# One projection block of a hybrid trunk, cut into eight pieces of k and placed inside the delta-rule scan's last chunk

## The chip, the cores and the metric

The kernel runs on one NeuronCore of a Trainium2 chip. Its time is the device time in microseconds (us) of one execution. All inputs are float32, and every matmul of this kernel appears in the trace as two instructions. Five engines work side by side, each with its own instruction queue, and wait for each other through semaphores: TensorE (PE; its weight loads are shown apart as PEld), VectorE (DVE), ScalarE (ACT), GpSimd (POOL) and SyncE (SP), which streams the weights.

## The reference

Two layers (`DEPTH = 2`), each on 512 latent and 128 context tokens (T = 640 columns) with D = 1024. What matters here, cut down:

```
h = rmsnorm(x, norm_mix_w[l]) * (1 + sc_a) + sh_a
(m_cq, m_ckv, m_kpe, g_q, g_k, g_v, g_z, g_a, g_b, hy_u, d_q, d_k, d_v, z_gate) = split(h @ w_in[l])
o_a = mla_attend(...m_cq, m_ckv, m_kpe...)       # latent attention
o_b, s_gdn = gdn_branch(...)                     # chunked gated delta rule, both directions
o_c = hyena_branch(...) ; o_d = diff_attend(...)

# inside gdn_branch, for each chunk of 64 tokens (kb = k*beta):
a_mat = I + strict_lower(kb k^T * decay)         # is inverted, here by doubling
v_new = u - w state ; o = q e^g state + intra v_new
state = state e^g_last + k^T v_new
# after the last chunk:
o_b = rmsnorm(o, norm_w) * silu(z)
x = x + gt_a * (sum_n sigmoid(gate_n) * (o_n @ w_branch[n])) @ w_out ; then a squared-ReLU MLP
```

## The kernel before

Activations lie transposed, 128 channels by 640 tokens. The input projection `h @ w_in` is cut into 24 blocks of 128 output channels. `win_block(l, n)` computes block n: it waits for its weights in one of four ring slots (`landed`), for the evacuation of an earlier block, and runs `dense`: for each of eight pieces of k (128 input channels each) one matmul over 512 and one over 128 columns, into one half of `psD`, a PSUM tile of two halves with two banks each. The last matmul raises `block_done`; ACT copies the half out (`evac` and its kin) and raises `dense_out`. Before, block n uses half `n % 2`. From block 2 on, block n waits for `dense_out` number n-1, which says that blocks 0 to n-2 have been copied out.

The order on every engine is the order in which the code is written. On PE a layer starts with `hyena` (blocks 0 to 7) and `gdn` (blocks 8 to 14), then come blocks 15 to 17 and `mla` (blocks 18 to 23).

Inside `gdn`, five scan steps (chunks) are worked off; steps 0 to 3 go in pairs, so that PE works on one while DVE works on the other. Step 4 is alone. For each step the inverse of a 64 x 64 lower triangle is made by doubling. A level k has, on PE, `lower_times(s, k)` (L1038); on DVE `w_masked` (L2234), which masks its result; on PE `inverse_times(s, k)` in two halves (L1050 and L1058), which waits for that; and on DVE `inverse_less` (L2244) and `turned_less` (L2254, for the last level L2263), which subtract them. `lower_times(s, k+1)` waits for `inverse_less(s, k)`. After level 5 come `corner_lower` (L1069), ACT's `corner_in` (L1703), `corner_inverse` (L1081) and ACT's `corner_out` (L1713).

The **tail** of step 4 is a chain: `new_values(4)` (L1107), ACT's copy `values_in` (L1718), `outputs(4)` (L1127 and L1133), and DVE's `collect(4)` (L2282, L2293), which raises `scan_done` number 5. The step uses `psA` for the doubling and half 0 of `psD` (`free_bank`, `out_bank`) for the tail. Half 1 of `psD` is in use by the scan (`pair_of`) until `query_keys(4)` has read it, which raises `at_ready` number 5, well ahead of step 4's doubling.

After `scan_done` PE runs block 14, then the **branch sum** (L1254, eight matmul instructions: the sum of squares for the branch's norm), then block 15. The **norm chain** starts at the branch sum: on ACT the logarithm (L1749), a table load and the exponential (L1750), on DVE two products (L2408, L2409); the second raises `gdn_done`. ACT waits for `gdn_done` before it evacuates block 14 (L1550), since the target lies in memory that the branch has used till then. Block 16 on PE waits for that evacuation, `dense_out` number 15:

```
            def mla(l):
                act.wait_ge(*gdn_done.nth(l, 1))
                act.wait_ge(*stored.nth(l, 1))
                evac(l, 14, m_cq[:, 0])
                evac(l, 15, m_cq[:, 1])
```

Of the kernel before, what the change touches and what calls it, by code (L numbers as in the profile page):

```python
# [17 lines left out]
ACT = mybir.ActivationFunctionType  # L18
# [4 lines left out]
KC = D // P  # L23
DEPTH = 2
LAT, CTX = 512, 128
T = LAT + CTX
# [3 lines left out]
KEYS = LAT + 128 + CTX  # L30
# [13 lines left out]
N_GROUP = 2 * KC + N_EARLY // GROUPS  # L44

BRANCHES = (1, 2, 0, 3)
N_FLOW = 24
PACK = 4
N_TURN = N_LATE + N_EARLY // PACK
# [88 lines left out]
def trunk(nc, ins, outs, links):  # L138
    ctx = ExitStack()
    with ctx:  # L140
# [327 lines left out]
        def length_banks(c):  # L468
            b = 2 * ((c + 1) % 2)
            return psA[:, b:b + 2, :].rearrange("p b n -> p (b n)")  # L470

        def tiles_of(s):

            return (s, 3 - s) if s < 4 else (4, 4)
# [246 lines left out]
        def _(pe):  # L721
            mm = nc.tensor.matmul

            def dense(out, j, rhs, ready=None):
                for k in range(KC):
                    if ready:
                        pe.wait_ge(*ready(k))
                    for a, b in SEGS:
                        last = mm(out[:, a:b], ring[:, j, k, :], rhs[:, k, a:b], start=k == 0, stop=k == KC - 1)  # L729
                return last  # L730
# [44 lines left out]
            def norm_sum(l, at_end):  # L775
# [5 lines left out]
                    last = mm(psD[:, 0, a:b], c_("ones"), h[:, KC - 1, a:b], start=False, stop=True)  # L781
                last.then_inc(sumsq_done.sem, 1)

            def win_block(l, n):

                j = n % RING
                landed(l, n)
                if n >= 2:
                    pe.wait_ge(*dense_out.nth(l, n - 1))
                dense(psD[:, n % 2], j, h, (lambda k: h_ready.nth(l, k + 1)) if n == 0 else None)\  # L790
                    .then_inc(block_done.sem, 1)

            for _ in range(RING):
# [128 lines left out]
            def gdn(l):  # L922
# [104 lines left out]
                def lower_times(s, k):  # L1027

                    i = s % 2
                    if k:  # L1030
                        held(pe, *xi_in[i].nth(l, turn_no(s, 6, k)))
                    else:
                        held(pe, *lt_ready.nth(l, s + 1))
                    for d, hh in units:
                        u = d * 4 + hh
                        for r in range(2):
                            mv = xi[i][rows(r), u] if k else c_("identc", rows(r))
                            last = mm(psA[rows(r), 2 * i, u * 64:(u + 1) * 64], lt[s % 3][rows(r), d, hh, rows(r)], mv,  # L1038
                                      start=True, stop=True)
                    last.then_inc(w_ps[i].sem, 1)  # L1040

                def inverse_times(s, k):

                    i = s % 2
                    held(pe, *wm_in[i].nth(l, turn_no(s, 6, k + 1)))
                    if k:
                        held(pe, *xt_in[i].nth(l, turn_no(s, 6, k)))
                        for u in range(8):
                            for r in range(2):
                                last = mm(psA[rows(r), 2 * i, u * 64:(u + 1) * 64], xt[i][rows(r), u], wm[i][rows(r), u],  # L1050
                                          start=True, stop=True)
                        last.then_inc(xi_ps[i].sem, 1)
                    elif s >= 2:
                        held(pe, *xtf_in.nth(l, s - 1))
                    for u in range(8):
                        for r in range(2):
                            mv = xt[i][rows(r), u] if k else c_("identc", rows(r))
                            last = mm(psA[rows(r), 2 * i + 1, u * 64:(u + 1) * 64], wm[i][rows(r), u], mv,  # L1058
                                      start=True, stop=True)
                    last.then_inc(xt_ps[i].sem, 1)  # L1060
# [170 lines left out]
                inverse_times(4, 1)  # L1231
                new_values(3)
                lower_times(4, 2)
                inverse_times(4, 2)
                outputs(3)
                lower_times(4, 3)
                inverse_times(4, 3)
                lower_times(4, 4)
                inverse_times(4, 4)
                lower_times(4, 5)  # L1240
                inverse_times(4, 5)
                corner_lower(4)
                corner_inverse(4)
                new_values(4)
                outputs(4)

                pe.wait_ge(*scan_done.nth(l, 5))
                win_block(l, 14)

                pe.wait_ge(*osq_ready.nth(l, 1))  # L1250
                for c in range(2):
# [272 lines left out]
            with pe.Fori(0, DEPTH) as l:  # L1524
                hyena(l)
                pe.wait_ge(*hy_done.nth(l, 1))
                gdn(l)
                win_block(l, 15)
                for n in range(16, 18):
                    win_block(l, n)  # L1530
                mla(l)
                attention(l)
                merge(l)
                out_proj(l)
                pe.wait_ge(*residual.nth(l, 7))
                norm_sum(l, 0)
                mlp(l)
                pe.wait_ge(*residual.nth(l, 39))
                norm_sum(l, 1)
# [3 lines left out]
        def _(act):  # L1543
# [3 lines left out]
            def evac(l, n, dst):  # L1547

                act.wait_ge(*block_done.nth(l, n + 1))
                a(dst, psD[:, n % 2, 0:T], ACT.Copy).then_inc(dense_out.sem, 1)  # L1550

            def evac_conv(l, n):

# [275 lines left out]
# [5 lines that stand above are left out]

                for n, dst in ((16, m_ckv), (17, kpe)):
                    act.wait_ge(*block_done.nth(l, n + 1))
                    a(dst[:, 0:LAT], psD[:, n % 2, 0:LAT], ACT.Copy)
                    a(dst[:, T:KEYS], psD[:, n % 2, LAT:T], ACT.Copy).then_inc(dense_out.sem, 1)
                act.wait_ge(*dense_out.nth(l, 18))
                a(m_sq[:, 0:2], m_cq, ACT.Square)  # L1840
                a(m_sq[:, 2, 0:LAT], m_ckv[:, 0:LAT], ACT.Square)
                a(m_sq[:, 2, LAT:T], m_ckv[:, T:KEYS], ACT.Square).then_inc(mla_sq.sem, 1)
                for n in (18, 19):
                    evac(l, n, d_q[:, n - 18])
                for n, wd in enumerate((256, 128)):
                    act.wait_ge(*mla_sum.nth(l, n + 1))
                    src = psA[:, 2 * n:2 * n + 2, :].rearrange("p b n -> p (b n)")[:, 0:T]
                    chain.link(a(m_rs[:, n], src, ACT.Ln, scale=1.0 / wd, bias=c_("eps")))
                for n in range(2):
                    a(m_rs[:, n], m_rs[:, n], ACT.Exp, scale=-0.5).then_inc(mla_rs.sem, 1)  # L1850
                for n in (20, 21):
                    act.wait_ge(*block_done.nth(l, n + 1))
                    a(d_k[:, n - 20, 0:LAT], psD[:, n % 2, 0:LAT], ACT.Copy)
                    a(d_k[:, n - 20, T:KEYS], psD[:, n % 2, LAT:T], ACT.Copy).then_inc(dense_out.sem, 1)
                for hh in range(H):
                    act.wait_ge(*mla_q_ps.nth(l, hh + 1))
                    a(m_q[0:96, hh], psD[0:96, hh % 2, 0:T], ACT.Copy).then_inc(mla_q_in.sem, 1)
                for hh in range(H):
                    act.wait_ge(*mla_k_ps.nth(l, hh + 1))
                    a(m_k[0:64, hh], psD[0:64, hh % 2, 0:KEYS], ACT.Copy).then_inc(mla_k_in.sem, 1)  # L1860
                for n in range(3):
                    act.wait_ge(*mla_v_ps.nth(l, n + 1))
                    a(m_v[:, 2 * n:2 * n + 2], psA[:, n, :].rearrange("p (t c) -> p t c", t=2), ACT.Copy)\
                        .then_inc(mla_v_in.sem, 1)
                a(d_k[:, :, LAT:T], p_("dk_c").rearrange("p (c t) -> p c t", c=2), ACT.Copy)
                a(d_v[:, 4], p_("dv_c"), ACT.Copy)
                act.wait_ge(*lam_sum.nth(l, 1))
                a(lam_s[:, 68:70], lam_s[:, 64:66], ACT.Exp).then_inc(lam_exp.sem, 1)
                act.wait_ge(*rot_in.nth(l, 1))
                a(m_k[64:96], kpe[64:96].unsqueeze(1).to_broadcast([32, H, KEYS]), ACT.Copy)\  # L1870
                    .then_inc(mla_k_rope.sem, 1)
                evac(l, 22, d_vf[:, 0])
                act.wait_ge(*rot_in.nth(l, 4))
                for c in range(KC):
                    a(h_high[:, c], h[:, c], ACT.Copy).then_inc(h_high_in.sem, 1)
                evac(l, 23, d_vf[:, 1])
                act.wait_ge(*stored.nth(l, 3))
                act.wait_ge(*rot_in.nth(l, 5))
                act.wait_ge(*mla_k_rope.nth(l, 1))
                high_part(l, B_GATE, 0)  # L1880
# [965 lines left out]
```

## Time and profile before

| what | value |
|---|---|
| median of 3 runs | 3095.86 us (3094.11 to 3096.72) |
| profiled execution, its own time | 3100.46 us |
| its span, first to last instruction | 3098.9 us |
| PE busy / PEld busy | 94% / 78% of the span |
| DVE / ACT / POOL busy | 34% / 26% / 21% |
| share of PE in the chain that ended last | 89% |
| mean granted TensorE clock | 0.976 of full speed |

The time of the profiled execution is 1.6 us longer than its span (what lies around the first and last instruction) and 4.6 us above the median of the runs without a profile. Times in the views are counted from the start of the span. "idle" in brackets is how long the engine stood before the row's first instruction, and behind the arrow stands the instruction that released it. PEclk 1.00 is 2.4 GHz, 0.50 is 1.2 GHz.

### The profile page before, as it was taken

The page shows a single profiled execution, that of the slowest core. Times are in us where ns is not written, and L with a number is a line of the kernel's source. Part 1 is how long each engine was busy: PE and PEld are TensorE (multiplying, and loading weights), DVE is VectorE, ACT ScalarE, POOL GpSimd, SP SyncE. Part 2 cuts the span into 40 slices and gives each one's busy share as a digit, 9 for nine tenths or more (in the row PEclk, how much of TensorE's full clock was granted, in tenths as well). Part 3 has the DMA queues.
Part 4 walks back from the last instruction along what each step waited for, and adds up shares of the span by engine and source line. Part 5 has one row for each costly group of instructions (what it writes and reads, how often), then busy time and mean ns, then how long its engine had stood idle before and what let it go on. Part 6 is the DMA issues. An engine that isn't in the chain of part 4 may idle for free.

```text
span 3098.9 us, 55916 instructions
## 1 busy us (share of the span) xinstructions
PE 2907.4 (94%) x23136; PEld 2426.2 (78%) x23136; DVE 1058.2 (34%) x1984; ACT 809.3 (26%) x1214; POOL 656.1 (21%) x428
## 2 busy tenths in 40 slices
PE   6999999999999899999989998999999998999997
PEld 3558855777778799999956697567777788999997
DVE  1546613224543331111244574132355324111113
ACT  2131023222331241221221411232233214221222
POOL 0102102111212323333301110021121122333332
PEclk9999999999999999999999999999999999999999
DMA  7110011222124222323230100112221232222222
GB/s 301 38 43 10 3 43 36 77 77 77 62 77 135 96 75 90 96 83 96 83 135 25 42 4 10 52 48 77 77 77 63 100 112 90 83 96 89 89 91 81
DMA packets 56671, 235.54 MB, mean 76 GB/s; under 512 B 6624, under 2 KB 6784, under 8 KB 55136
## 3 DMA queue, kind: packets, MB, share of 16 engines
q1 hardware_dynamic: 53568, 206.67, 20.2%
q0 software_dynamic: 2848, 25.13, 2.2%
q8 instruction: 202, 3.31, 0.4%
q14 instruction: 53, 0.43, 0.0%
HBM read 222.96 MB, written 8.81 MB: 75 GB/s over the span
## 4 chain that ended last, share of the span: by engine, by line
PE 89%; DVE 4%; issue 3%; ACT 2%; DMA 1%; POOL 0%; SPq 0%; DVEq 0%; POOLq 0%; ACTq 0%
PE ps_dense L736 47%; PE ps_dense L729 13%; PE ps_dense L1261 4%; PE ps_aux L1312 3%; PE ps_dense L1333 2%; PE ps_aux L1058 2%; PE ps_aux L1038 2%; PE ps_aux L1050 2%; PE ps_aux L1261 1%; PE ps_aux L759 1%; DMA w_ring<-in_w_early 1%; PE ps_dense L1324 1%; PE ps_dense L759 1%; PE ps_dense L1107 1%; PE ps_dense L1399 1%
## 5 line engine op out<-in xcount | busy, mean ns | idle before, releaser
L657 POOL TENSOR_TENSOR w_low<-w_ring,w_high 128x1024 fp32r<-128x1024 f32 x208 | 512.6, 2465 | 1089.4 <-ACT w_high L1566 1087.9
L736 PE MATMUL ps_dense<-h_high,w_high 128*128 128x320 f32 x2048 | 491.8, 321 | 55.5 <-DVE h_low L1979 21.8
L736 PE MATMUL ps_dense<-h_high,w_low 128*128 128x320 f32 x2048 | 468.9, 310 | 0.0
L736 PE MATMUL ps_dense<-h_low,w_high 128*128 128x320 f32 x2048 | 468.7, 310 | 0.0
L729 PE MATMUL ps_dense<-h_norm,w_ring 128*128 128x512 f32 (+1 forms) x1536 | 434.7, 444 | 18.7 <-ACT h_norm L1591 10.6
L729 PEld LDWEIGHTS ps_dense<-h_norm,w_ring 128*128 128x128 f32 x1536 | 240.3, 195 | 217.7 <-issue 206.7
L736 PEld LDWEIGHTS ps_dense<-h_high,w_high 128*128 128x128 f32 x2048 | 336.5, 190 | 79.1 <-issue 44.0
L1566 ACT ACTIVATE w_high<-w_ring 128x1024 fp32r<-128x1024 f32 x208 | 218.9, 1053 | 534.2 <-PE ps_dense L736 433.5
L736 PEld LDWEIGHTS ps_dense<-h_low,w_high 128*128 128x128 f32 x2048 | 344.9, 189 | 0.0
L736 PEld LDWEIGHTS ps_dense<-h_high,w_low 128*128 128x128 f32 x2048 | 344.4, 189 | 0.0
L736 PE MATMUL ps_dense<-z_high,w_high 128*128 128x320 f32 x1280 | 296.5, 313 | 13.5 <-POOL w_low L657 13.5
L736 PE MATMUL ps_dense<-z_low,w_high 128*128 128x320 f32 x1280 | 293.8, 311 | 0.0
L736 PE MATMUL ps_dense<-z_high,w_low 128*128 128x320 f32 x1280 | 293.3, 310 | 0.0
L736 PEld LDWEIGHTS ps_dense<-z_high,w_high 128*128 128x128 f32 x1280 | 215.1, 190 | 16.9 <-issue 16.9
L736 PEld LDWEIGHTS ps_dense<-z_low,w_high 128*128 128x128 f32 x1280 | 216.0, 190 | 0.0
L736 PEld LDWEIGHTS ps_dense<-z_high,w_low 128*128 128x128 f32 x1280 | 215.9, 189 | 0.0
L2545 DVE SCALAR_TENSOR_TENSOR x_res<-ps_dense,mod,x_res 128x320 f32<-128x320 f32 (+2 forms) x192 | 72.6, 434 | 343.2 <-PE ps_dense L736 343.2
L2615 DVE CAST z_high<-flow 128x640 fp32r<-128x640 f32 x64 | 31.6, 494 | 390.3 <-ACT flow L1909 390.3
L2446 DVE TENSOR_REDUCE att_s<-ps_aux 128x1 f32<-128x640 f32 (+1 forms) x120 | 86.2, 718 | 193.4 <-PE ps_aux L1312 161.4
L1907 ACT ACTIVATE flow<-ps_dense 128x640 f32<-128x640 f32 x64 | 45.1, 705 | 321.0 <-PE ps_dense L736 321.0
L1261 PE MATMUL ps_dense<-bout,w_ring 128*128 128x128 f32 (+1 forms) x384 | 115.6, 444 | 0.0
L1261 PEld LDWEIGHTS ps_dense<-bout,w_ring 128*128 128x128 f32 x384 | 61.8, 191 | 45.9 <-issue 45.9
(390 smaller groups left out, 3237.7 us busy)
## 6 DMA issues: line engine op xcount, KB each, us to landing
w_ring<-in_w_mlp SPq DMA_DIRECT2D x128, 512.0 KB, 3.7
w_ring<-in_w_gate SPq DMA_DIRECT2D x64, 640.0 KB, 3.9
w_ring<-in_w_late SPq DMA_DIRECT2D x64, 512.0 KB, 4.6
w_ring<-in_w_early SPq DMA_DIRECT2D x48, 512.0 KB, 3.7
w_ring<-in_w_in SPq DMA_DIRECT2D x48, 512.0 KB, 3.6
w_ring<-in_w_out SPq DMA_DIRECT2D x16, 512.0 KB, 3.7
arena<-in_dft POOLq DMA_DIRECT2D x2, 3264.0 KB, 13.1
par<-in_par POOLq DMA_DIRECT2D x3, 1731.0 KB, 7.6
```

The lines of the kernel that those rows point to most:

```text
L657: g.tensor_tensor(w_low[:, n % 2], ring[:, slot, 0:KC, :], w_high[:, n % 2].bitcast(F32), ALU.subtract).then_inc(w_low_in.sem, 1)
L729: last = mm(out[:, a:b], ring[:, j, k, :], rhs[:, k, a:b], start=k == 0, stop=k == KC - 1)
L736: last = mm(psD[:, b, s * 512:s * 512 + HALF], w_[:, par_, k, :], x_[:, k, s * HALF:(s + 1) * HALF], start=k == 0 and x_ is x_high and w_ ...
L759: last = mm(out[32 * (k % 4):32 * (k % 4) + 32], cond_pad[:, k, at:at + 32], ring[:, slot, k, :], start=j == 0 and k < 4, stop=j == of - 1 ...
L1038: last = mm(psA[rows(r), 2 * i, u * 64:(u + 1) * 64], lt[s % 3][rows(r), d, hh, rows(r)], mv, start=True, stop=True)
L1050: last = mm(psA[rows(r), 2 * i, u * 64:(u + 1) * 64], xt[i][rows(r), u], wm[i][rows(r), u], start=True, stop=True)
L1058: last = mm(psA[rows(r), 2 * i + 1, u * 64:(u + 1) * 64], wm[i][rows(r), u], mv, start=True, stop=True)
L1261: last = mm(out[:, a:c], ring[:, 2 * i % RING, KC + k, :], bout[:, BRANCHES[i // KC], k, a:c], start=k == 0, stop=k == 1)
L1312: last = mm(out[:, a:b], qt, k[:, a:b], start=True, stop=True)
L1566: a(w_high[:, n % 2], ring[:, j, 0:KC, :], ACT.Copy).then_inc(w_high_in.sem, 1)
L2446: link(v.tensor_reduce(small_[:, 2 * m, u:u + 1], src, AX.X, ALU.max, negate=True))
L2545: last = v.scalar_tensor_tensor(out=dst[:, p:q], in0=ps, scalar=gate[:, s:s + 1], in1=dst[:, p:q], op0=ALU.mult, op1=ALU.add)
```

## The change

Block 14 is no longer run after `scan_done`. A new function `win_piece(l, k)` runs its piece k, two matmuls, and the eight pieces are put between PE's parts of step 4: pieces 0, 1, 3 and 5 between a `lower_times` and its `inverse_times`; pieces 2, 4 and 6 between an `inverse_times` and what follows; piece 7 between `corner_lower` and `corner_inverse`. Block 15 takes block 14's place after `scan_done`; nothing takes block 15's place after the branch sum. Since the scan's tail uses half 0 of `psD`, block 14 now goes to half 1: `slot_of` gives block 14 and all later blocks the other half than before. Block 15 waits for no evacuation any more; blocks 16 and later wait as before.

```
+N_SCAN_BLOCK = 14
...
+        def slot_of(n):
+
+            return n % 2 if n < N_SCAN_BLOCK else (n + 1) % 2
...
+            def win_piece(l, k):
+
+                n = N_SCAN_BLOCK
+                if k == 0:
+                    landed(l, n)
+                    pe.wait_ge(*dense_out.nth(l, n))
+                    pe.wait_ge(*at_ready.nth(l, 5))
+                for a, b in SEGS:
+                    last = mm(psD[:, slot_of(n), a:b], ring[:, n % RING, k, :], h[:, k, a:b], start=k == 0, stop=k == KC - 1)
+                if k == KC - 1:
+                    last.then_inc(block_done.sem, 1)
...
-                if n >= 2:
+                if n > N_SCAN_BLOCK + 1:
                     pe.wait_ge(*dense_out.nth(l, n - 1))
-                dense(psD[:, n % 2], j, h, (lambda k: h_ready.nth(l, k + 1)) if n == 0 else None)\
+                elif n >= 2 and n < N_SCAN_BLOCK:
+                    pe.wait_ge(*dense_out.nth(l, n - 1))
+                dense(psD[:, slot_of(n)], j, h, (lambda k: h_ready.nth(l, k + 1)) if n == 0 else None)\
...
                 lower_times(4, 2)
+                win_piece(l, 0)
                 inverse_times(4, 2)
                 outputs(3)
                 lower_times(4, 3)
+                win_piece(l, 1)
                 inverse_times(4, 3)
+                win_piece(l, 2)
                 lower_times(4, 4)
+                win_piece(l, 3)
                 inverse_times(4, 4)
+                win_piece(l, 4)
                 lower_times(4, 5)
+                win_piece(l, 5)
                 inverse_times(4, 5)
+                win_piece(l, 6)
                 corner_lower(4)
+                win_piece(l, 7)
                 corner_inverse(4)
                 new_values(4)
                 outputs(4)
 
                 pe.wait_ge(*scan_done.nth(l, 5))
-                win_block(l, 14)
+                win_block(l, 15)
...
                 gdn(l)
-                win_block(l, 15)
                 for n in range(16, 18):
                     win_block(l, n)
```

On the other engines only the half that ACT reads changes (`psD[:, slot_of(n)]` for `psD[:, n % 2]`).

PE's queue at levels 3 and 4 of step 4 before (`lower_times`, `inverse_times` in two halves, then the next level; the names in brackets are the semaphores waited for, `inverse_w_in0` is DVE's mask, `inverse_in0` DVE's subtraction):

```order
L1038 MATMUL ps_aux<-arena 64x64 [waits inverse_in0]
L1038 MATMUL ps_aux<-arena 64x64 x15
L505 REGISTER_ALU
L1050 MATMUL ps_aux<-arena 64x64 [waits inverse_w_in0,inverse_turned_in0]
L1050 MATMUL ps_aux<-arena 64x64 x15
L1058 MATMUL ps_aux<-arena 64x64 x16
L1038 MATMUL ps_aux<-arena 64x64 [waits inverse_in0]
L1038 MATMUL ps_aux<-arena 64x64 x15
```

The same place in the changed kernel, where L1057, L1069 and L1077 are the lines of L1038, L1050 and L1058, and L797 is a piece:

```order
L1057 MATMUL ps_aux<-arena 64x64 [waits inverse_in0]
L1057 MATMUL ps_aux<-arena 64x64 x15
L797 MATMUL ps_dense<-h_norm,w_ring 128x512
L797 MATMUL ps_dense<-h_norm,w_ring 128x128
L510 REGISTER_ALU
L1069 MATMUL ps_aux<-arena 64x64 [waits inverse_w_in0,inverse_turned_in0]
L1069 MATMUL ps_aux<-arena 64x64 x15
L1077 MATMUL ps_aux<-arena 64x64 x16
L797 MATMUL ps_dense<-h_norm,w_ring 128x512
L797 MATMUL ps_dense<-h_norm,w_ring 128x128
L1057 MATMUL ps_aux<-arena 64x64 [waits inverse_in0]
L1057 MATMUL ps_aux<-arena 64x64 x15
```

One piece now stands where PE waited for the mask, and one where the next level followed at once.

PE's queue behind the scan before: the last two matmuls of the branch sum, then block 15, which waits for block 13's evacuation, then block 16:

```order
L1254 MATMUL ps_aux<-arena,con 128x512
L1254 MATMUL ps_aux<-arena,con 128x128
L729 MATMUL ps_dense<-h_norm,w_ring 128x512 [waits dense_out,ring_in3]
L729 MATMUL ps_dense<-h_norm,w_ring 128x128
...
L753 ISA
L789 REGISTER_ALU [waits ring_in0]
L729 MATMUL ps_dense<-h_norm,w_ring 128x512 [waits dense_out]
L729 MATMUL ps_dense<-h_norm,w_ring 128x128
```

The same place in the changed kernel (L1281 is the branch sum, L734 is `dense`):

```order
L1281 MATMUL ps_aux<-arena,con 128x512
L1281 MATMUL ps_aux<-arena,con 128x128
L758 ISA
L806 REGISTER_ALU [waits ring_in0]
L734 MATMUL ps_dense<-h_norm,w_ring 128x512 [waits dense_out]
L734 MATMUL ps_dense<-h_norm,w_ring 128x128
```

Block 16, with its wait for block 14's evacuation, now stands directly behind the branch sum.

## Rows read from the trace of the kernel before

**Rows 1.** The page's head, and its fourth part, the chain by engine.
```profile
span 3098.9 us, 55916 instructions
...
PE 89%; DVE 4%; issue 3%; ACT 2%; DMA 1%; POOL 0%; SPq 0%; DVEq 0%; POOLq 0%; ACTq 0%
```
**Rows 2.** PE in order of time, doubling of step 4, layer 1: start us, us, instructions, [idle before].
```profile
377.19 1.15 PE L1050 MATMUL ps_aux<-arena 64*64 64x64 f32 x32 [1.04 <-DVE arena L2234]
...
379.21 1.15 PE L1038 MATMUL ps_aux<-arena 64*64 64x64 f32 x32
...
387.61 0.68 PE L1069 MATMUL ps_aux<-arena 64*64 64x64 f32 x16
389.24 0.68 PE L1081 MATMUL ps_aux<-arena 64*64 64x64 f32 x16 [0.95 <-DVE arena L2263]
```
**Rows 3.** DVE in order of time, the mask ahead of the first row above.
```profile
376.21 0.69 DVE L2234 TENSOR_TENSOR arena<-ps_aux,con 128x512 f32<-128x512 f32 x1 [0.33 <-PE ps_aux L1038]
```
**Rows 4.** PE in order of time, layer 1, the two parts of `outputs` at full clock.
```profile
358.07 1.16 PE L1133 MATMUL ps_dense<-arena,bout 128*128 128x128 f32 x8
...
373.99 1.09 PE L1127 MATMUL ps_dense<-arena 128*64 128x128 f32 x16
```
**Rows 5.** PE in order of time, layer 1, tail of step 4 and what follows.
```profile
390.77 3.43 PE L1107 MATMUL ps_dense<-bout,arena 128*128 128x64 f32 x16 [0.86 <-ACT arena L1713]
394.99 1.98 PE L1127 MATMUL ps_dense<-arena 128*64 128x128 f32 x16 [0.78 <-ACT arena L1718]
...
400.78 10.85 PE L729 MATMUL ps_dense<-h_norm,w_ring 128*128 128x512 f32 x32 [1.81 <-DVE bout L2293]
...
413.63 43.43 PE L729 MATMUL ps_dense<-h_norm,w_ring 128*128 128x512 f32 x160
```
**Rows 6.** PE in order of time, the same places in layer 2.
```profile
1910.41 2.00 PE L1107 MATMUL ps_dense<-bout,arena 128*128 128x64 f32 x16 [0.86 <-ACT arena L1713]
1913.19 1.80 PE L1127 MATMUL ps_dense<-arena 128*64 128x128 f32 x16 [0.78 <-ACT arena L1718]
...
1918.79 8.91 PE L729 MATMUL ps_dense<-h_norm,w_ring 128*128 128x512 f32 x32 [1.81 <-DVE bout L2293]
...
1929.70 43.43 PE L729 MATMUL ps_dense<-h_norm,w_ring 128*128 128x512 f32 x160
```
**Rows 7.** ACT and DVE in order of time, the norm chain and block 14's evacuation.
```profile
413.83 1.33 ACT L1749 ACTIVATE arena<-ps_aux,con 128x1280 f32<-128x1280 f32 x1 [10.58 <-PE ps_aux L1254]
...
419.37 1.49 DVE L2409 TENSOR_TENSOR bout<-bout,arena 128x1280 f32<-128x1280 f32 x1
...
421.07 0.70 ACT L1550 ACTIVATE arena<-ps_dense 128x640 f32<-128x640 f32 x1 [3.33 <-DVE bout L2409]
...
1937.14 0.70 ACT L1550 ACTIVATE arena<-ps_dense 128x640 f32<-128x640 f32 x1 [3.32 <-DVE bout L2409]
```
**Rows 8.** Stretches: us, busy (instructions) of PE, PEld, DVE, ACT, POOL, PEclk, DMA.
```profile
369.00:391.00 22.00, 16.07 (x440) 14.89 (x437) 9.71 (x15) 1.55 (x4) 0.00 (x0) 1.00 0.01 2
391.30:404.50 13.20, 10.61 (x44) 8.05 (x44) 2.48 (x5) 3.15 (x3) 0.61 (x1) 0.50 0.03 11
...
1913.80:1916.50 2.70, 2.70 (x19) 2.37 (x16) 0.00 (x0) 0.00 (x0) 0.00 (x0) 0.50 0.00 0
...
931.70:937.20 5.50, 5.50 (x26) 3.02 (x26) 0.29 (x1) 0.70 (x1) 0.00 (x0) 0.50 0.00 0
...
1574.20:1578.40 4.20, 4.18 (x7) 2.12 (x8) 3.87 (x6) 4.20 (x8) 0.00 (x0) 0.50 0.16 68
```
**Rows 9.** PE in order of time, first work after two long waits.
```profile
931.66 1.08 PE L759 MATMUL ps_aux<-w_ring,cond_pad 128*32 128x128 f32 x16 [5.59 <-DVE bout L2497]
...
1574.22 10.02 PE L729 MATMUL ps_dense<-h_norm,w_ring 128*128 128x512 f32 x27 [8.14 <-ACT h_norm L1591]
```
**Rows 10.** Weight loads in order of time, at the start of block 15.
```profile
413.52 0.30 PEld L729 LDWEIGHTS ps_dense<-h_norm,w_ring 128*128 128x128 f32 x2
```

More of the change, by code:

```diff
@@ L1549, in evac @@
                 act.wait_ge(*block_done.nth(l, n + 1))
-                a(dst, psD[:, n % 2, 0:T], ACT.Copy).then_inc(dense_out.sem, 1)
+                a(dst, psD[:, slot_of(n), 0:T], ACT.Copy).then_inc(dense_out.sem, 1)
             def evac_conv(l, n):
@@ L1836, in mla @@
                     act.wait_ge(*block_done.nth(l, n + 1))
-                    a(dst[:, 0:LAT], psD[:, n % 2, 0:LAT], ACT.Copy)
-                    a(dst[:, T:KEYS], psD[:, n % 2, LAT:T], ACT.Copy).then_inc(dense_out.sem, 1)
+                    a(dst[:, 0:LAT], psD[:, slot_of(n), 0:LAT], ACT.Copy)
+                    a(dst[:, T:KEYS], psD[:, slot_of(n), LAT:T], ACT.Copy).then_inc(dense_out.sem, 1)
                 act.wait_ge(*dense_out.nth(l, 18))
@@ L1852, in mla @@
                     act.wait_ge(*block_done.nth(l, n + 1))
-                    a(d_k[:, n - 20, 0:LAT], psD[:, n % 2, 0:LAT], ACT.Copy)
-                    a(d_k[:, n - 20, T:KEYS], psD[:, n % 2, LAT:T], ACT.Copy).then_inc(dense_out.sem, 1)
+                    a(d_k[:, n - 20, 0:LAT], psD[:, slot_of(n), 0:LAT], ACT.Copy)
+                    a(d_k[:, n - 20, T:KEYS], psD[:, slot_of(n), LAT:T], ACT.Copy).then_inc(dense_out.sem, 1)
                 for hh in range(H):
```

## The prediction

> **What bounds the kernel now.** I read the page first: PE holds 89% of the chain that ended last [rows 1]. So a change of PE's order is worth what it takes off PE's waits, less what it adds to PE's work on a chain. Next I read PE in order of time around step 4. There the chain alternates between two engines. `lower_times` ends, DVE masks its result (0.69 us, [rows 3]), and PE starts the next half 1.04 us after it went idle [rows 2]. This wait stands ahead of each `inverse_times` of levels 2 to 5, and one of 0.95 us stands between the two corners [rows 2]. Between `inverse_times` and the next `lower_times` there is no wait: the row of L1038 at 379.21 has no idle time before it. Then the tail: PE waits 0.86, 0.78 and 1.81 us between its parts [rows 5, 6]. Last, behind the scan, PE runs from 413.63 on without a pause through blocks 15 to 19 [rows 5]. It is this that the change touches most, so I read ACT and DVE beside it: the norm chain starts at 413.83, its last product ends at 420.86, and block 14's evacuation ends at 421.77 [rows 7].
>
> **The removed block.** Block 14's 16 matmuls leave the stretch after `scan_done`. A block at full clock takes 43.43 / 5 = 8.69 us [rows 5]. Taking the whole of it as a saving would be wrong. Only one block now stands between `scan_done` and the branch sum, as before, so the branch sum comes no sooner from that. Behind the branch sum block 15 used to run while the norm chain ran. Block 16 cannot start before block 14's evacuation has ended (421.77), whatever PE does, and ACT does that one only after `gdn_done`. With 0.14 us from an ACT end to a PE start (the tail's copy ends at 394.85, L1127 starts at 394.99; I read the same 0.14 in the second layer) block 16 starts at 421.91. Before, it started when block 15 ended: 413.63 + 8.69 = 422.32. So the whole block saves 0.41 us here, and in the second layer 1929.70 + 8.69 = 1938.39 against 1937.14 + 0.70 + 0.14 = 1937.98, again 0.41 us [rows 6, 7]. In place of block 15, PE idles for 8.1 us (413.80 to 421.91).
>
> **The pieces.** A piece is an eighth of a block, 1.086 us. Pieces 0, 1, 3 and 5 fill waits of 1.04 us and cost about 0.05 each, 0.2 together. Piece 7 fills 0.95 us and costs 0.14. Pieces 2, 4 and 6 stand where PE had no wait, and nothing hides them: what DVE owes the next `lower_times` was ready when PE got there. They cost 3 x 1.086 = 3.26. Together 3.6 us a layer. What the trace doesn't show is a 128 x 128 weight load directly behind 64 x 64 work. The nearest row is the start of block 15, where two loads take 0.30 us, 0.11 of it ahead of the first matmul [rows 10]. Bounds: nothing, or 0.19 us (most of one load) at each of eight pieces, 1.5 us. I take 0.05 a piece, since the load can go ahead while the 64 x 64 work drains: 4.0 us a layer, between 3.3 (if the ends of matmuls overlap a little more than the trace models) and 5.1. What waits behind a piece on PE is only the doubling itself. The piece's own waits (weights, `dense_out` 14, `at_ready` 5) were met long before. SP gets `block_done` 14 some 20 us sooner and loads the ring slot sooner, behind nothing that waits for it. ACT's order is unchanged: it still waits for `gdn_done` before both evacuations. The exchange of halves costs nothing: blocks 16 to 23 keep their distance to their evacuations, and what follows block 23 waits for all of them.
>
> **The clock before the branch sum.** In layer 1 the clock stood at 1.00 through the doubling, then at 0.50 from about 391.2 to 404.6, after the corners' and the tail's waits [rows 8]. What that cost is read against layer 2, where L1107 ran at full clock: from its start to L1127's start 4.22 us against 2.78 (1.4); L1127 and L1133 to their end at 398.97, 3.98 us against 1.02 + 1.16 = 2.18 (1.8; L1127 at full clock starts at 373.99 and the next row at 375.01) [rows 4 to 6]; block 14 10.85 against 8.69 (2.2). That is 5.4 us. In layer 2 the half clock covered only L1127 and L1133 (1913.8 to 1916.5, [rows 8]): 3.79 against 2.18 is 1.6, with 0.2 in the block 1.8 us. The pieces raise PE's work during the doubling (16.07 of 22 us before) and fill the wait between the corners. They leave the tail's three waits as they are. Layer 2 shows that such a tail loses the clock even when it enters at full speed. So I expect the cost that layer 2 had, 1.8 us, in both layers: a gain of 3.6 in the first, nothing in the second. The bounds are no loss of clock at all (gains 5.4 and 1.8) and the long stretch in both (0 and a loss of 3.6).
>
> **The clock after the branch sum.** This is a new cost. PE now stands 8.1 us ahead of block 16. The trace has waits of that kind: after 5.59 us the work from 931.66 ran at 0.50 until past 937.2, and after 8.14 us the work from 1574.22 until past 1578.4 [rows 8, 9]. Work at half clock for 4.3 to 5.7 us loses half of it, 2.2 to 2.9 us. I take 2.6 a layer, with 1.7 to 3.0 as bounds.
>
> The Trainium skill, TensorE: Matmul & The Clock Gate, section "Loop structure matters more than you think", says that a long wait between groups of matmuls lets the clock drop and the next group runs cold; this speaks against the change, and by it alone the 8.1 us hole costs as the rows say. The trace agrees: both long waits above were followed by 0.50.
>
> **The sum.** Layer 1: +4.0 - 3.6 - 0.4 + 2.6 = +2.6. Layer 2: +4.0 + 0 - 0.4 + 2.6 = +6.2. Together +8.8 us. Against the profiled execution's own 3100.46 us that gives 3109.3. That execution lies 4.6 us above the median of the runs, so the median goes to about 3095.86 + 8.8 = 3104.7 us. The likeliest case's own range is +4.5 to +13.
>
> **The rivals.**
> *The clock holds to the branch sum.* The filled waits keep PE busy enough that neither tail loses the clock. For it: the doubling ran at 1.00 even with its waits, and it now has almost none. Against it: layer 2's tail. Sum: layer 1 4.0 - 5.4 - 0.4 + 2.6 = +0.8, layer 2 4.0 - 1.8 - 0.4 + 2.6 = +4.4, together +5.2: 3101.1 us. The Trainium skill, same page, section "What's actually happening", has it that the throttled state is the default and activity releases it; read so, more activity ahead of the tail gives this case. The trace bears it out only in part, since the clock fell at 391.2 behind a well filled doubling.
>
> *The pieces cost more and the clock less.* Weight loads are exposed (5.1 a layer) and the gain of 3.6 in layer 1 doesn't come: 2 x 5.1 - 0.8 + 5.2 = +14.6: 3110.5 us. For it: every piece changes the shape on PE twice. Against it: a load can run beside earlier matmuls.
>
> *The removed block comes off.* If block 16 did not have to wait for the norm chain, each layer would save 8.69 us in place of 0.41, and would have no hole to pay for: layer 1 4.0 - 3.6 - 8.7 = -8.3, layer 2 4.0 - 8.7 = -4.7, together -13.0: 3082.9 us. The place is the wait for `dense_out` 15. It decides from the point where the norm chain with the evacuation takes less than 8.69 - 4.0 = 4.7 us; it takes 8.1 [rows 7]. Against it: the evacuation's row names L2409 as its releaser.
>
> **How the numbers follow.** Chances: the forecast 0.50, the clock holds 0.22, dearer pieces 0.24, the block comes off 0.04. A measurement of this kernel tells about 0.2%, 6.2 us, from no change. The forecast is slower in 0.43 of its 0.50 and within 0.2% in the rest; the second case is within in 0.17 of 0.22 and slower in 0.05, the third always slower, the last faster in 0.03. Rounded: faster 0.03, within 0.2% 0.25, slower 0.72. The range reaches from below the second case to above the third, +2.6 to +16: 3098.5 to 3112.
>
> **What would show it.** Right: in the changed profile PE's rows show no idle time ahead of `inverse_times` of levels 2 to 5; step 4 from its level 2 to the corner's end is 3.3 to 5.1 us longer; a PE idle of about 8 us stands ahead of block 16 with block 14's evacuation as releaser; and PEclk is 0.50 at its start. Wrong: block 16 starts soon after the branch sum; or the clock stays at 1.00 behind the hole (then the sum is +3.6); or the tail of layer 1 keeps its long stretch at 0.50 (then +12.4).

## The result, and the profile after

The changed kernel takes 3104.55 us (median of 11 runs, 3099.58 to 3111.95) against 3095.86 us before (11 runs): ratio 1.0031, 95% interval 1.0022 to 1.0041, which is 7 to 13 us slower. The forecast was 3104.7 us. One run of a kernel further down (waits_only) took 3589.73 us at a granted clock of 0.776, where its eleven others took 3089.72 to 3098.26 us, and stands in no ratio.

PE of the changed kernel in order of time, both layers (start us, us, instructions, idle before). L797 is a piece, L1057, L1069, L1077 are the lower product and the two halves behind it, L1088 and L1100 the corners, L1126 the new values, L1281 the branch sum, L734 a dense block, L1407 the sum of squares behind block 19:

```profile
366.90 2.00 PE L1126 MATMUL ps_dense<-bout,arena 128*128 128x64 f32 x16
368.83 1.15 PE L1057 MATMUL ps_aux<-arena 64*64 64x64 f32 x32
369.91 1.35 PE L797 MATMUL ps_dense<-h_norm,w_ring 128*128 128x512 f32 x4
371.19 1.15 PE L1069 MATMUL ps_aux<-arena 64*64 64x64 f32 x32
...
378.65 1.10 PE L1077 MATMUL ps_aux<-arena 64*64 64x64 f32 x32
379.68 1.35 PE L797 MATMUL ps_dense<-h_norm,w_ring 128*128 128x512 f32 x4
380.96 1.15 PE L1057 MATMUL ps_aux<-arena 64*64 64x64 f32 x32
...
392.24 0.68 PE L1088 MATMUL ps_aux<-arena 64*64 64x64 f32 x16
392.86 1.35 PE L797 MATMUL ps_dense<-h_norm,w_ring 128*128 128x512 f32 x4
394.13 0.68 PE L1100 MATMUL ps_aux<-arena 64*64 64x64 f32 x16
395.68 2.00 PE L1126 MATMUL ps_dense<-bout,arena 128*128 128x64 f32 x16 [0.87 <-ACT arena L1739]
398.46 1.09 PE L1146 MATMUL ps_dense<-arena 128*64 128x128 f32 x16 [0.78 <-ACT arena L1744]
...
402.38 8.92 PE L734 MATMUL ps_dense<-h_norm,w_ring 128*128 128x512 f32 x32 [1.74 <-DVE bout L2319]
411.13 2.33 PE L1281 MATMUL ps_aux<-arena,con 128*128 128x512 f32 x8
421.49 36.40 PE L734 MATMUL ps_dense<-h_norm,w_ring 128*128 128x512 f32 x128 [8.03 <-ACT arena L1576]
457.73 3.41 PE L1407 MATMUL ps_aux<-arena,con 128*128 128x512 f32 x12
...
1882.38 2.00 PE L1126 MATMUL ps_dense<-bout,arena 128*128 128x64 f32 x16
...
1911.16 2.00 PE L1126 MATMUL ps_dense<-bout,arena 128*128 128x64 f32 x16 [0.87 <-ACT arena L1739]
...
1926.61 2.33 PE L1281 MATMUL ps_aux<-arena,con 128*128 128x512 f32 x8
...
1973.23 3.41 PE L1407 MATMUL ps_aux<-arena,con 128*128 128x512 f32 x12
```

Three things are to be seen. The wait ahead of `inverse_times` is gone [rows 2], but the piece there takes from 369.91 to 371.19, 1.28 us and not an eighth of a block (1.09). Where no wait was (379.68 to 380.96) it costs these 1.28 us whole. And block 16 (421.49) starts 8.03 us after the branch sum, released by L1576.

ACT of the changed kernel says what L1576 waited for:

```profile
413.50 1.33 ACT L1775 ACTIVATE arena<-ps_aux,con 128x1280 f32<-128x1280 f32 x1 [8.57 <-PE ps_aux L1281]
...
420.74 1.30 ACT L1576 ACTIVATE arena<-ps_dense 128x640 f32<-128x640 f32 x2 [3.33 <-DVE bout L2435]
```

It is the second product of the norm chain, as before [rows 7]; now both evacuations follow at once.

Stretches of the changed kernel (us, busy time of PE, PEld, DVE, ACT, POOL, PEclk, DMA): tail and block 15; the hole; block 16's start; behind it.

```profile
395.70:411.00 15.30, 12.79 (x71) 8.49 (x72) 2.48 (x5) 3.15 (x3) 0.61 (x1) 1.00 0.11 40
...
413.50:421.40 7.90, 0.00 (x0) 0.00 (x0) 2.99 (x2) 4.54 (x5) 0.00 (x0) 0.77 0.11 42
421.50:424.80 3.30, 3.30 (x6) 1.76 (x7) 0.00 (x0) 0.54 (x1) 0.00 (x0) 0.53 0.00 0
425.00:435.00 10.00, 10.00 (x39) 5.63 (x38) 0.00 (x0) 0.77 (x2) 0.00 (x0) 1.00 0.17 48
```

In this execution the tail held 2.4 GHz in both layers, and the clock fell inside the hole: the mean of 0.53 over block 16's first 3.3 us means 3.1 us at half clock.

To add up, I take **the stretch**: from the new values of step 3 (366.90 here) to the sum of squares behind block 19 (457.73). All that the change moves lies in it. The rows that bound it before, and the branch sums between them:

```profile
366.44 2.34 PE L1107 MATMUL ps_dense<-bout,arena 128*128 128x64 f32 x16
...
411.47 2.33 PE L1254 MATMUL ps_aux<-arena,con 128*128 128x512 f32 x8
...
456.90 3.41 PE L1380 MATMUL ps_aux<-arena,con 128*128 128x512 f32 x12
...
1886.41 2.00 PE L1107 MATMUL ps_dense<-bout,arena 128*128 128x64 f32 x16
...
1927.54 2.33 PE L1254 MATMUL ps_aux<-arena,con 128*128 128x512 f32 x8
...
1972.97 3.41 PE L1380 MATMUL ps_aux<-arena,con 128*128 128x512 f32 x12
```

Both layers together it takes 177.02 us before and 181.68 us after, 4.7 us more. Yet the span of this execution is 0.9 us shorter than that of the profiled execution before (3098.0 against 3098.9 us). The rest of the program, which the change doesn't touch, was 5.6 us faster, and most of that is the clock elsewhere. Four short stretches with half clock before are at 2.4 GHz in the changed kernel, and one that was not has it (at 248 us). Two of the four, before:

```profile
1694.50:1697.50 3.00, 3.00 (x9) 1.73 (x8) 2.93 (x4) 1.26 (x2) 0.00 (x0) 0.58 0.00 0
...
2019.50:2022.50 3.00, 3.00 (x5) 1.50 (x6) 2.86 (x6) 2.36 (x1) 0.00 (x0) 0.50 0.00 0
```

and in the changed kernel:

```profile
1694.50:1697.50 3.00, 3.00 (x13) 1.68 (x12) 2.93 (x7) 0.74 (x1) 0.00 (x0) 1.00 0.00 0
...
2019.50:2022.50 3.00, 3.00 (x11) 1.70 (x11) 2.90 (x5) 2.62 (x1) 0.00 (x0) 1.00 0.00 0
```

So whole profiled executions can't be set against each other here. Over three traces of each kernel the rest of the program took 2916.9 to 2921.9 us before and 2914.0 to 2922.4 in the changed kernel: it scatters by up to 8 us, and neither kernel has the shorter one. The stretch can be compared, and so can the medians of many runs.

### The profile page after: what moved, and what is told of

The parts are those of the page before. It is cut to its first block, busy times and chain, and to the rows that moved or that the text cites. A ratio compares the mean times of both kernels' runs of the same rounds, so it can differ in the third digit from the quotient of the medians.

```text
span 3098.0 us, 55914 instructions
## 1 busy us (share of the span) xinstructions
PE 2903.1 (94%) x23136; PEld 2422.2 (78%) x23136; DVE 1058.4 (34%) x1984; ACT 809.3 (26%) x1214; POOL 656.9 (21%) x428
## 4 chain that ended last, share of the span: by engine, by line
PE 89%; DVE 4%; issue 3%; ACT 3%; DMA 1%; POOL 0%; SPq 0%; DVEq 0%; POOLq 0%; ACTq 0%
PE ps_dense L741 47%; PE ps_dense L734 13%; PE ps_dense L1288 4%; PE ps_aux L1339 3%; PE ps_dense L1360 2%; PE ps_aux L1077 2%; PE ps_aux L1057 2%; PE ps_aux L1069 2%; PE ps_aux L1288 1%; PE ps_aux L764 1%; DMA w_ring<-in_w_early 1%; PE ps_dense L1351 1%; PE ps_dense L764 1%; PE ps_dense L797 1%; PE ps_dense L1126 1%
## 5 line engine op out<-in xcount | busy, mean ns | idle before, releaser
L734 PE MATMUL ps_dense<-h_norm,w_ring 128*128 128x512 f32 x1472 | 414.8, 443 | 34.3 <-ACT arena L1576 16.1
L734 PEld LDWEIGHTS ps_dense<-h_norm,w_ring 128*128 128x128 f32 x1472 | 229.3, 195 | 224.4 <-issue 193.3
```

## The experiments

My theory: the removed block saves nothing much since the norm chain sets block 16's start; the pieces cost several us a layer; the clock gives back part ahead of the branch sum and takes some behind it. Rivals: the hole is the main cost; or the pieces are all of it and the clock gives nothing. The time of each kernel is to be read by its ratio to the kernel before, run on the same chip (there it took 3097.31 us beside left_out, extra_pieces, hole_filled and sum_first, and 3094.83 us beside the last four). "Stretch" is that of both layers in its trace.

| kernel | median us | ratio, 95% interval | stretch us |
|---|---|---|---|
| before, three traces | 3095.86 | | 177.02, 176.67, 176.98 |
| change, three traces | 3104.55 | 1.0031, 1.0022 to 1.0041 | 181.68, 185.25, 185.34 |
| left_out | 3097.68 | 1.0002, 0.9993 to 1.0011 | 175.15 |
| extra_pieces | 3133.27 | 1.0119, 1.0103 to 1.0134 | 179.46 |
| hole_filled | 3133.06 | 1.0122, 1.0104 to 1.0140 | 178.58 |
| sum_first | 3087.88 | 0.9971, 0.9958 to 0.9983 | 172.81 |
| waits_only | 3094.95 | 1.0001, 0.9991 to 1.0010 | 174.85 |
| waits_sum_first | 3077.92 | 0.9947, 0.9934 to 0.9960 | 160.08 |
| swap_only | 3094.60 | 1.0001, 0.9992 to 1.0011 | 176.84 |
| nops_added | 3095.03 | 0.9999, 0.9990 to 1.0009 | 176.92 |

**left_out: what is the removed block worth?**

```
-                win_piece(l, 0)      (and 1 to 6)
-                win_piece(l, 7)
+                landed(l, N_SCAN_BLOCK)
+                pe.nop().then_inc(block_done.sem, 1)
```

> The changed kernel without block 14's matmuls at all (the block is left out of the computation, its signal is raised by an empty instruction at piece 7's place). Theory: behind the scan the norm chain and not PE sets when block 16 starts, so that leaving out 17.4 us of PE work (two layers) saves 0.8 us against the kernel before, and the hole ahead of block 16 then costs 1.6 to 2.6 us a layer through the clock: 2.4 to 4.4 us slower than the kernel before, about 3099 us. Rival, the removed block comes off: 17 us faster than before, 3079 us. Rival, the hole costs nothing: 0.8 us faster than before.

Measured: as fast as the kernel before (2 us faster to 3 us slower). So 17.4 us of PE's work fewer, and no gain. The rival that the block comes off (17 us faster) is refuted. The low end of what I expected, 2.4 us slower, lies within the interval. The stretch is 1.9 us shorter than before, where I expected it longer. The hole isn't the reason, since its clock costs 1.4 to 1.5 us a layer here, near the 1.6 behind that 2.4. It is the tails: both lost about 1.6 us (17.06 and 17.00 us from the new values to the branch sum, 15.45 at full clock), where before one of them lost 5.2. PE of this kernel in order of time:

```profile
399.99 8.92 PE L734 MATMUL ps_dense<-h_norm,w_ring 128*128 128x512 f32 x32 [1.74 <-DVE bout L2313]
408.74 2.33 PE L1275 MATMUL ps_aux<-arena,con 128*128 128x512 f32 x8
419.10 36.26 PE L734 MATMUL ps_dense<-h_norm,w_ring 128*128 128x512 f32 x128 [8.03 <-ACT arena L1570]
```

The hole is the same 8.03 us.

**extra_pieces: the pieces alone.** Blocks 14 and 15 stay where they were before, and `win_piece` does work that is done a second time. (Left out of the excerpt: the pieces raise no signal, and `slot_of` is `n % 2` throughout.)

```
-                win_block(l, 15)
+                win_block(l, 14)
...
                 gdn(l)
+                win_block(l, 15)
```

> The kernel before with the eight pieces added as extra work (they compute block 14 a second time into a half that is overwritten), so that nothing is taken away behind the scan and there is no hole. Theory: the pieces lengthen step 4 by 4.8 us a layer (9.5 us), and the clock gives back between nothing and the 7.2 us that the tails and block 14 lost in the profiled execution of before: 2.5 to 9.5 us slower than before, most likely 5. Rival, the hole is the main cost of the change: not over 3 us slower than before. Rival, the pieces are the whole cost and the clock gives nothing: 9.5 us slower, as much as the change.

**hole_filled: the hole's clock.** Left out of the excerpt: on ACT, block 15's evacuation waits for the last of the added matmuls.

```
                 last.then_inc(osum_ps.sem, 1)
+                for k in range(14):
+                    last = mm(psD[:, 0, T:T + 320], c_("ones"), h[:, k % KC, 0:320], start=True, stop=True)
+                last.then_inc(osum_ps.sem, 1)
```

> The changed kernel with 14 matmuls of 320 columns (7.5 us, results unused) behind the branch sum, where PE has its hole of 8.0 us. Theory: block 16 then starts at full clock and not later than before, which saves 1.6 us a layer by the trace of the changed kernel (up to 2.6): 3 to 5 us faster than the change, 4 to 6 us slower than before. Rival, the clock behind the hole does not matter: the same time as the change, 8.7 us slower than before.

Both missed by far, 36 us slower than before and not 2 to 10. But not in the stretch. There extra_pieces took 179.46 us, 2.4 to 2.8 more than before. This total alone doesn't part the theory (2.5 to 9.5) from the rival that the hole is the main cost (not over 3), but its parts do: from one new values to the next it takes 28.78 us in both layers, 4.8 a layer over full clock, and its tails, 15.52 us each, kept the clock and gave 6.8 us back. hole_filled took 178.58 us, 3.1 less than the first trace of the change, whose tails also kept the clock, and block 16 started no later (10.36 us behind the start of the branch sum in both). In the rows of hole_filled, block 16 to the sum of squares takes 453.27 - 418.56 = 34.71 us, against 457.73 - 421.49 = 36.24 in the change: the half clock behind the hole costs 1.53 us a layer.

```profile
418.56 34.88 PE L734 MATMUL ps_dense<-h_norm,w_ring 128*128 128x512 f32 x128 [0.49 <-ACT arena L1579]
453.27 3.41 PE L1410 MATMUL ps_aux<-arena,con 128*128 128x512 f32 x12
```

The 36 us lie in the MLP, hundreds of us away. Its loop runs four times a layer, and early in the second to fourth pass PE stood 2.5 to 3.3 us with no releaser (1.9 to 3.1 in hole_filled). PE of extra_pieces in order of time:

```profile
1213.21 0.45 PE L741 MATMUL ps_dense<-h_high,w_low 128*128 128x320 f32 x2 [2.78 <-issue]
...
1334.92 0.69 PE L741 MATMUL ps_dense<-h_high,w_low 128*128 128x320 f32 x2 [2.71 <-issue]
...
1458.15 0.69 PE L741 MATMUL ps_dense<-h_high,w_low 128*128 128x320 f32 x2 [3.25 <-issue]
```

and its clock behind the first two of them, in stretches:

```profile
1213.30:1216.50 3.20, 3.20 (x14) 3.20 (x14) 0.00 (x0) 0.00 (x0) 0.00 (x0) 0.54 0.00 0
1334.90:1339.80 4.90, 4.88 (x19) 4.88 (x19) 0.00 (x0) 0.00 (x0) 0.00 (x0) 0.50 0.02 5
```

Six such waits make 17.8 us, and 3.4 to 4.9 us of work at half clock behind each some 13 us more; with the stretch that is 33 us. The median is 36 us slower, and the span of this execution 27 to 32 us longer than those of the kernel before, so the sum has the right size but does not close exactly.

The traces say where these waits stand. In extra_pieces PE stops 0.85 us after each pass has begun, behind four matmul instructions, in all six passes; in hole_filled 1.58 us after, behind nine. So the stop has a fixed place in PE's program, and the place moves with the code that was added ahead of the loop. The DMA queue named q8 instruction (16 KB a packet) fits to it: in both kernels the last packet ahead of each of the twelve resumptions landed 1.2 to 1.5 us before PE went on. The first ran from 1210.89 to 1211.77, and PE went on at 1213.21. This speaks for PE having waited for its instructions. It is argued and not shown, since no run moves the loop's body without adding matmuls.

The kernel before and the changed one have no such second wait. They have waits with no releaser ahead of a pass's first matmul, where in the other passes PE waits as long or longer for DVE: one to five before (1.2 to 5.8 us together), three to five in the changed kernel (3.4 to 5.6), none over 1.2 us. So they are no part of its 8.7 us.

**nops_added: is it the length of PE's program?**

```
+                for _ in range(60):
+                    pe.nop()
                 pe.wait_ge(*hy_done.nth(l, 1))
```

> The kernel before with 60 empty instructions on PE, where PE waits for the Hyena branch to end. Tests why the two kernels with 14 and 16 matmuls more than the change were 36 us slower: their traces show eight waits of about 3 us inside the MLP loop with no releaser, far from the added work. Theory A, where PE's loop body lies among its instructions decides (instruction supply): the empty instructions move it too, and the kernel is 15 to 35 us slower. Theory B, the added matmuls themselves do it (work or clock): the same time as before, at most 1 us more.

Measured: no difference. That doesn't refute theory A. The profile counts 55916 instructions, as before, and has no row at the line of the empty ones, so it is not shown that they reached the program. For theory A speaks what the traces of the two slow kernels say above; a test that moves the loop's body is missing.

**swap_only: the exchange of halves alone.** ACT's reads change with it (left out of the excerpt).

```
+            return n % 2 if n < N_SCAN_BLOCK else (n + 1) % 2
...
-                dense(psD[:, n % 2], j, h, (lambda k: h_ready.nth(l, k + 1)) if n == 0 else None)\
+                dense(psD[:, slot_of(n)], j, h, (lambda k: h_ready.nth(l, k + 1)) if n == 0 else None)\
```

> The kernel before with only the halves exchanged from block 14 on; order and pieces as before. Theory: the exchange costs nothing, within 2 us of before (noise of the clock). Rival, the exchange changes who waits for which evacuation: over 3 us slower.

Measured: no difference, and a stretch of 176.84 us. The exchange costs nothing.

**before_again, before_third, after_again, after_third: how steady is the clock?** No edit.

> The kernel before once more, for a second trace. If the half clock of the first layer's tail (13 us in the first trace) is usual, it stands here again and costs about 5 us; if not, the tail costs 1 to 2 us as in the second layer, and the change gains less from the clock than the first trace let expect.

> The changed kernel once more, for a second trace. If its tails hold the clock by their work, both stand at full clock again (15.45 us from the new values to the branch sum); if that was chance, one of them loses 1 to 3 us. The hole of 8.0 us and a half clock at block 16's start must be there again.

> The kernel before a third time, same question as the second trace.

> The changed kernel a third time, same question as its second trace.

From the last new values to the branch sum takes 15.45 us at full clock. Before, in all three traces, one layer took 17.1 and the other 20.6 to 20.7: the long loss of 5.2 us is usual, in layer 1 in the first trace and in layer 2 in the others. swap_only and nops_added show the same, 17.1 in one layer and 20.7 in the other. Together the tails lose 6.8 to 6.9 us each time. The changed kernel lost nothing in its first trace and 3.6 us in layer 1 in the other two (its layer 2 held). PE of after_again in order of time:

```profile
398.32 2.10 PE L1126 MATMUL ps_dense<-bout,arena 128*128 128x64 f32 x16 [0.87 <-ACT arena L1739]
401.19 1.97 PE L1146 MATMUL ps_dense<-arena 128*64 128x128 f32 x16 [0.78 <-ACT arena L1744]
403.10 2.08 PE L1152 MATMUL ps_dense<-arena,bout 128*128 128x128 f32 x8
406.91 10.58 PE L734 MATMUL ps_dense<-h_norm,w_ring 128*128 128x512 f32 x32 [1.73 <-DVE bout L2319]
417.33 2.33 PE L1281 MATMUL ps_aux<-arena,con 128*128 128x512 f32 x8
```

Its outputs and the block behind take nearly what they took before in layer 1 [rows 5]. So the stretch of the change is 181.7 or 185.3 us, 4.7 or 8.3 us more than before.

**sum_first: block 15 back under the norm chain, the pieces as they are.**

```
                 pe.wait_ge(*scan_done.nth(l, 5))
-                win_block(l, 15)
                 pe.wait_ge(*osq_ready.nth(l, 1))
...
                 last.then_inc(osum_ps.sem, 1)
+                win_block(l, 15)
```

> The changed kernel with block 15 behind the branch sum again, so that nothing but the square on ACT stands between the scan and the branch sum. Theory: the branch sum starts 8.7 us sooner less some 1.5 us of waiting for the square, the norm chain then runs under block 15 as before, and there is no hole: 4.8 us for the pieces less 7.2 us a layer, 2.4 us a layer faster than before, together about 5 us, 3091 us, and some us less or more by the clock of the tail. Rival, the norm chain is not what block 16 waits for (another wait takes its place): no faster than the change.

Measured: 9 us faster than before (5 to 13). The rival is refuted: with nothing changed but the order, 8.7 us slower turns into 9 us faster. Its stretch, 172.81 us, is 4 us shorter than before and 9 to 12.5 shorter than that of the change; the clock fell in or behind both tails of this trace (6.8 us at half in the first layer, 13.6 in the second). The other 5 us of the median this one trace doesn't show, and the eleven runs lie far apart (3077.71 to 3096.09 us).

**waits_only: pieces only where PE waited.**

```
                 inverse_times(4, 3)
-                win_piece(l, 2)
                 lower_times(4, 4)
-                win_piece(l, 3)
+                win_piece(l, 2)
                 inverse_times(4, 4)
...
                 corner_lower(4)
+                win_piece(l, 4)
                 corner_inverse(4)
+                win_piece(l, 5)
                 new_values(4)
+                win_piece(l, 6)
                 outputs(4)
+                win_piece(l, 7)
```

> The changed kernel with its eight pieces only where PE waited: behind the lower products of levels 2 to 5, between the corners, behind the second corner (0.86 us of wait), between the new values and the outputs (0.78) and behind the outputs (1.81). Theory: a piece takes 1.28 us in place and adds 0.18, 0.26, 0.36, 0.43 and 0 us in these waits, 1.8 us a layer in place of 4.8, and the hole behind the branch sum stays: 6 us faster than the change, 1 to 4 us slower than the kernel before. Rival, a piece costs its whole length wherever it stands: the same as the change.

Measured: as fast as the kernel before, so 9 us faster than the change, a little better than expected. PE in order of time:

```profile
392.83 1.90 PE L1126 MATMUL ps_dense<-bout,arena 128*128 128x64 f32 x16
394.57 1.30 PE L797 MATMUL ps_dense<-h_norm,w_ring 128*128 128x512 f32 x4
...
399.71 8.92 PE L734 MATMUL ps_dense<-h_norm,w_ring 128*128 128x512 f32 x32 [0.66 <-DVE bout L2319]
```

From one new values to the next it takes 25.24 us in both layers, against 28.78 in the change and 24.0 before at full clock, and the tail 15.64 in place of 15.45: the eight pieces cost 1.4 us a layer, not 4.8. Its tails kept the clock in this trace.

**waits_sum_first: both.**

> Both together: pieces only where PE waited, and block 15 behind the branch sum, so that it runs under the norm chain. Theory: 6 us faster than block 15 behind the branch sum with the pieces of the change, which was 9 us faster than before: 13 to 16 us faster than before, 3081 to 3084 us. Rival, the clock: with nothing dense ahead of the branch sum it falls in the tail more often and takes back part: 10 us faster than before.

Measured: 3077.92 us (five runs, 3077.50 to 3078.90), 17 us faster than before (12 to 20). PE in order of time:

```profile
396.54 2.40 PE L1279 MATMUL ps_aux<-arena,con 128*128 128x512 f32 x8 [2.05 <-ACT arena L1771]
398.77 43.43 PE L734 MATMUL ps_dense<-h_norm,w_ring 128*128 128x512 f32 x160
442.04 3.41 PE L1406 MATMUL ps_aux<-arena,con 128*128 128x512 f32 x12
```

The branch sum waits 2.05 us for the square, block 15 follows it at once, and there is no hole. The stretch is 17 us shorter than before, which is the whole gain. The rival with the clock (10 us) did not come: in this trace PE ran at half clock for 3.4 us in the second layer (from 1904.5) and not at all in the first.

## Why the prediction was right, and where it was not

**The removed block.** Right: forecast 0.41 us a layer, and from the branch sum to block 16 it takes 10.36 us where the sum and block 15 took 2.16 + 8.69 = 10.85 before, 0.49 us saved. left_out shows the same with no pieces in the way.

**The pieces.** The mechanism was right, the size too small: forecast 4.0 us a layer (bounds 3.3 and 5.1), measured 28.78 - 24.0 = 4.8. The part mis-sized is the weight load and the change of shape around a piece, for which I took 0.05 us a piece; in place a piece takes 1.28 us and not 1.09, 0.19 more, which is what my upper bound assumed. The three pieces where PE had not waited cost 3.8 us of the 4.8, the four ahead of `inverse_times` 0.18 each (368.83 to 371.19 is 2.36 us, 375.01 to 377.19 was 2.18 before), and the one between the corners 0.26. Which part of the 0.19 is the weight load and which the change of shape, no run shows.

**The clock before the branch sum.** This is the step that was right in its total alone, and in two traces of three. Forecast a gain of 3.6 us in all. Measured 6.9 us in the first trace, and 3.2 to 3.3 in the other two. The first is the rival in which the clock holds, the others have the size of the forecast, but not its split: I expected 1.8 us lost in each layer, and it was 3.6 in the first and nothing in the second. In these two traces layer 1 kept a long loss (the clock at half from 400.1 to 410.3 in after_again), which I had named as a sign of being wrong; that layer 2 lost nothing made up for it, and that was luck. What decides which of the two an execution gets isn't shown. I had also read the loss before a little too high, 5.4 and 1.8 us where it was 5.2 and 1.7: I set a block's row against 8.69 us, but the row of a single block is 8.92 us at full clock too (402.38), as it ends with its last matmul.

**The clock behind the branch sum.** Right in kind, too large: forecast 2.6 us a layer, measured 1.53. The rows I took it from had work at half clock for 4.3 to 5.7 us [rows 8, 9]; behind this hole it was 3.1 us.

**The sum.** Measured terms: 2 x (4.8 - 0.5 + 1.5) = 11.6 us, less 3.3 or 6.9 us of clock, 8.3 or 4.7 us. Two traces of three lie at 8.3, the medians differ by 8.7, with 7 to 13 as their interval. That the forecast of 8.8 came out so near was luck: a term too small by 1.6 us (pieces) and one too large by 2.1 us (hole) nearly cancelled. The direction was not: the uncovered norm chain, the pieces where PE had not waited and the half clock behind the hole were each forecast and found.

**The rivals.** That the block comes off is refuted by left_out. Dearer pieces (10.2 us for both layers) came nearly true for the pieces, 9.5, but without the rest of that case. The signs of being right were all there: the waits ahead of `inverse_times` gone, step 4 longer by 4.8 us, a hole of 8 us released by block 14's evacuation, and half clock behind it. Of the signs of being wrong one came in part, the long loss in layer 1's tail.

## What to carry to other kernels

Before work is moved out of a place, look what ran beside it: block 15 was cover for a chain of 8 us on two other engines, and shifting it up by one place uncovered that chain, so that the block taken away was worth 0.5 us and not 8.7. Move filler into waits that the trace shows, reckon with its length in place (here 1.28 us for a wait of 1.04), and keep it out of places where the engine never waited. Where the half clock comes and goes, compare a stretch that holds the change, and leave whole executions to many runs.

## What the runs showed of the hardware

- A pair of matmuls with 128 x 128 weights among 64 x 64 ones took 1.28 us, in a row of its own kind 1.09. Whether the weight load or the change of shape makes the difference isn't shown.
- The same kernel's stretch came out at one of two lengths 3.6 us apart (181.68, and 185.25 and 185.34), by whether the clock fell in a tail with three waits of 0.87, 0.78 and 1.74 us.
- A stand of 8.03 us was followed by 3.1 us of work at half clock, which cost 1.53 us; with matmuls in the hole the same four blocks took 34.71 us and not 36.24.
- Waits of 0.86, 0.78 and 1.81 us with short matmuls between them were enough for the clock to fall: the tails before lost 5.2 us in one layer and 1.7 in the other, in each of three traces.
- With fourteen or sixteen matmuls more in a layer's loop PE stood 1.9 to 3.3 us early in later passes of another loop, six times, and the kernel took 36 us more. Each stand began at the same place of PE's program and ended 1.2 to 1.5 us after a packet of the instruction queue had landed. That it waited for instructions is likely and not proven.
